# Two-layer decoder trunk on one core: norms summed block by block through PSUM banks, and attention's projection units placed in late row blocks and at head ends

## The reference, cut to what matters

```python
mod = silu(c) @ ada_w[l] + ada_b[l]          # sh1, sc1, g1, sh2, sc2, g2
h = rmsnorm(x, norm_g[l, 0]) * (1 + sc1) + sh1
y = even_mixer(h, ...) if l % 2 == 0 else odd_mixer(h, ...)
x = x + (1 + g1) * rmsnorm(y, norm_g[l, 1])
h = rmsnorm(x, norm_g[l, 2]) * (1 + sc2) + sh2
y = (silu(h @ w_gate) * (h @ w_up)) @ w_down
x = x + (1 + g2) * rmsnorm(y, norm_g[l, 3])
```

## Time and profile before

| | us |
|---|---|
| three runs | 2991.14 to 2992.17 |
| their median | 2991.62 |
| the profiled execution | 2992.33 |
| its span in the profile | 2990.6 |
| mean granted clock of PE | 0.947 of full |

### The profile page before, as it was taken

How to read it: one execution, slowest core, us unless ns; L and a number is a source line. 1 busy time by engine, 2 the same in 40 slices (tenths; PEclk the granted TensorE clock), 3 DMA queues, 4 the chain that set the end, 5 groups by cost and what they waited for, 6 DMA issues and landing times.

```text
span 2990.6 us, 35461 instructions
## 1 busy us (share of the span) xinstructions
PE 2687.0 (90%) x12576; PEld 2193.1 (73%) x12576; DVE 1261.9 (42%) x1451; ACT 1071.0 (36%) x1610; POOL 967.4 (32%) x402
## 2 busy tenths in 40 slices
PE   4999999989899999999999997666889999999995
PEld 2777778767678887788877786554667888788884
DVE  5566644333720155201567413766473005430145
ACT  2444443343433333333332223544343333322222
POOL 0111110004344444344434443211334444344442
PEclk7999999999899999999999998888999999999998
DMA  6233332043223332232346543111222333233232
GB/s 235 64 99 105 107 92 78 29 167 101 71 84 98 97 93 91 84 98 92 98 134 225 185 160 106 43 56 42 71 71 87 96 98 98 84 98 97 92 99 91
DMA packets 91097, 300.38 MB, mean 100 GB/s; under 512 B 9793, under 2 KB 10113, under 8 KB 91009
## 3 DMA queue, kind: packets, MB, share of 16 engines
q1 hardware_dynamic: 91008, 299.20, 31.4%
HBM read 275.05 MB, written 24.12 MB: 100 GB/s over the span
## 4 chain that ended last, share of the span: by engine, by line
issue 57%; PE 27%; POOL 11%; DVE 2%; DVEq 1%; ACT 1%; POOLq 1%; ACTq 0%
POOL w_lo L462 10%; PE ps L503 6%; PE ps L504 6%; PE ps L507 6%; PE ps L774 3%; PE ps L780 3%; PE ps L777 3%; POOL ybuf L473 1%; POOL arena L473 1%; DVEq L1222 0%; POOLq L476 0%; DVEq L1494 0%; DVE h_lo L1194 0%; ACT w_hi L828 0%; DVE ybuf L1186 0%
## 5 line engine op out<-in xcount | busy, mean ns | idle before, releaser
L462 POOL TENSOR_TENSOR w_lo<-w_raw,w_hi 128x1024 fp32r<-128x1024 f32 x370 | 909.4, 2461 | 1797.6 <-ACT w_hi L828 1293.5
L503 PE MATMUL ps<-h_hi,w_hi 128*128 128x512 f32 x2448 | 991.0, 405 | 85.8 <-ACT w_hi L828 54.7
L504 PE MATMUL ps<-h_lo,w_hi 128*128 128x512 f32 x2448 | 977.5, 399 | 0.0
L503 PEld LDWEIGHTS ps<-h_hi,w_hi 128*128 128x128 f32 x2448 | 474.6, 194 | 216.8 <-issue 78.3
L507 PE MATMUL ps<-h_hi,w_lo 128*128 128x512 f32 x2448 | 606.9, 390 | 0.0
L828 ACT ACTIVATE w_hi<-w_raw 128x1024 fp32r<-128x1024 f32 x346 | 363.9, 1057 | 632.0 <-PE ps L507 320.8
L504 PEld LDWEIGHTS ps<-h_lo,w_hi 128*128 128x128 f32 x2448 | 475.7, 194 | 97.0 <-issue 0.5
L507 PEld LDWEIGHTS ps<-h_hi,w_lo 128*128 128x128 f32 x2448 | 461.5, 189 | 96.4
L1598 DVE TENSOR_TENSOR arena<-arena,ps 128x512 f32 (+1 forms) x88 | 60.5, 688 | 782.6 <-PE ps L507 782.6
L1613 DVE TENSOR_TENSOR a_lo<-arena,a_hi 128x512 fp32r<-128x512 f32 x88 | 211.6, 2404 | 212.8 <-ACT a_hi L1149 212.5
L774 PE MATMUL ps<-a_hi,w_hi 128*128 128x512 f32 x704 | 174.3, 390 | 6.6 <-ACT a_hi L1149 6.6
(11 more groups left out here) (174 smaller groups left out, 2267.8 us busy)
## 6 DMA issues: line engine op xcount, KB each, us to landing
w_raw<-weights SPq DMA_DIRECT2D x370, 512.0 KB, 3.5
arena<-ada_w SPq DMA_DIRECT2D x80, 512.0 KB, 3.6
proj<-arena SPq DMA_DIRECT2D x24, 512.0 KB, 3.4
x<-xT SPq DMA_DIRECT2D x4, 2048.0 KB, 11.1
arena<-ada_w SPq DMA_DIRECT2D x4, 2048.0 KB, 20.2
arena<-proj SPq DMA_DIRECT2D x8, 1024.0 KB, 4.8
arena<-proj SPq DMA_DIRECT2D x8, 512.0 KB, 4.1
y_hi_d<-a_hi SPq DMA_DIRECT2D x7, 512.0 KB, 2.6
```

The costliest lines, as they stand in the source:

```text
L462: pool.tensor_tensor(w_lo[:, s, :], w_raw[:, s, :], w_hi[:, s, :].bitcast(f32), ALU.subtract).then_inc(lo_done, 1)
L503: pe.matmul(bank(b), w, high[:, k, :], start=k == 0, stop=False)
L504: pe.matmul(bank(b), w, low[:, k, :], start=False, stop=False)
```

## The change

- **Norms.** ACT squares each block of 512 columns into banks 6 and 7 in turn (`squares`); DVE adds each bank into acc_b (`sums`) and signals that it was read; block k waits until block k-2 was read. A square of x waits for its pair of blocks to be updated. `update` goes in four pairs: two scalar_tensor_tensor y·gain·rinv into banks 4 and 5, then one add of 1024 columns to x; `scaled` is gone. In the hosted stages the squares of the pre norm move from hook 3 to hooks 2 and 3, four blocks each; the second half of the update and sums 0 to 3 stand at DVE's hook 2, in that order.
- **Out.** ACT copies w_hi for unit m+2, squares and evicts all eight banks; POOL sums the squares (`out_norms`); DVE does reciprocal, update, sums and h. The post mean stands after unit 0 and the pre mean after unit 4 of half 1.
- **Down.** The first row begins with banks 4 to 7 and waits for free banks before bank 0; the last row goes bank by bank, three matmuls each, and signals each bank. After FFN(1,1) ACT squares banks as they finish, DVE adds, and the last update is shared by DVE and POOL.
- **Attention.** Chunks 0 to 3 stay in rows 0 to 3; chunk 4 is cut into three parts of 8 matmuls in rows 5, 6 and 7; chunk 5 stands whole after weigh(7). Scores 0 and 1 of the next block come before `turn_out`, `turn_v` after it. `ada_turn` of blocks 1 to 6 becomes a column after each matmul pair of chunk 0 of a later block. DVE's ada steps leave rows 0 and 1 and stand doubled in rows 2 and 3.

```diff
+                for half in range(2):
+                    done = 2 * layer + half
+                    for m in range(KB):
+                        use = USE_OUT[layer] + KB * half + m + 2
+                        lo(use, use % 2)
+                        if m:
+                            pool.wait_ge(ysq_done, 8 * done + m + 1)
+                            pool.tensor_tensor(acc_y[half], acc_y[half], sq_tile[m % 2], ALU.add).then_inc(ysq_read, 1)
+                            pool.drain()
+                    pool.drain().then_inc(yacc_done, 1)
...
+                    if ada is not None:
+                        ada_column(ada, k)
...
+            def chunk_part(c, part):
+
+                u, half = chunk_of(c)
+                if part == 0:
+                    chunk_bank_free(c)
+                    pe.wait_ge(hi_done, u + 1)
+                if part == 2:
+                    pe.wait_ge(lo_done, u + 3)
+                w, h = ((w_hi, hh), (w_hi, hl), (w_lo, hh))[part]
+                for k in range(KB):
+                    mm = pe.matmul(bank(7), w[:, u % 2, k * P:(k + 1) * P], h[half][:, k, :],
+                                   start=part == k == 0, stop=part == 2 and k == KB - 1)
+                if part == 2:
+                    mm.then_inc(ch_done, 1)
...
+                if m == 0:
+                    pe.wait_ge(acc_done, n + 1)
+                    pe.wait_ge(mod_done, n)
+                    pe.wait_ge(o_done, 8 * n + 1)
+                mm = pe.matmul(bank(6)[:, ADA_COL + m:ADA_COL + m + 1], acc_one[:, m * P:(m + 1) * P], ones[:, 0:1], start=True, stop=True)
+                if m == KB - 1:
+                    mm.then_inc(ada_mm, 1)
...
                                 mean(*post[0])
-                            if pre and (i, s) == (PAIRS_OUT - 1, 0):
+                            if pre and (i, s) == (2, 0):
                                 mean(*pre)
...
-                pe.wait_ge(ssum_done, n - 1)
+                if kind == 1:
+                    pe.wait_ge(yacc_done, 2 * layer + half + 1)
+                else:
+                    pe.wait_ge(bsum_done, 10 if (layer, kind, half) == (1, 3, 1) else square_site(layer, kind, half) + 1)
                 pe.wait_ge(root_done, n)
-                pe.matmul(bank(7), mean_w[:, :], rinv[:, rinv_slot(kind, half), :], start=True, stop=True)\
+                pe.matmul(bank(7), mean_w[:, :], acc_y[half] if kind == 1 else acc_b, start=True, stop=True)\
                     .then_inc(mean_done, 1)
...
+                        if n == 7 and not last:
+                            chunk_part(ahead + 4, 2)
                         if n:
...
                         turn_weights(n)
+                        if n == 7:
+                            chunk_part(ahead + 4, 2)
                         if n:
                             weigh(n - 1)
...
-                    if n < 6 and not last:
-                        chunk(6 * (b + 1) + n)
-                        if (b, n) == (6, 5):
-                            pe.drain().then_inc(unit_used, 24)
+                    if not last:
+                        if n < 4:
+                            chunk(ahead + n, b if n == 0 and 0 < b < 7 else None)
+                        elif n in (5, 6):
+                            chunk_part(ahead + 4, n - 5)
+                if not last:
+                    scores(0, b + 1, 1 - slot)
                 weigh(7)
                 if not last:
-                    turn_v(b + 1, before(LANE[kind]))
-                    scores(0, b + 1, 1 - slot)
+                    for part in range(3):
+                        chunk_part(ahead + 5, part)
+                    if b == 6:
+                        pe.drain().then_inc(unit_used, 24)
+                    scores(1, b + 1, 1 - slot)
                 turn_out()
+                if not last:
+                    turn_v(b + 1, before(LANE[kind] + 1))
...
+                def row(i, s, order=range(KB), first=False):
                     u = use + 2 * i + s
                     slot = (use + s) % 2
...
-                    for m in range(KB):
+                    for m in order:
+                        if first and m == 0:
+                            pe.wait_ge(free0, tiles + 1)
+                            pe.wait_ge(free1, tiles + 1)
                         pe.matmul(bank(m), w_hi[:, slot, cols[m]], a_hi[:, s, :], start=first, stop=False)
...
+                def last_row():
+
+                    u, slot = use + FB - 1, (use + 1) % 2
+                    pe.wait_ge(hi_done, u + 1)
+                    pe.wait_ge(ah_done, FB * (d + 1))
+                    pe.wait_ge(al_done, FB * (d + 1))
+                    pe.wait_ge(lo_done, u + 3)
+                    for j, m in enumerate(LAST_BANKS if d == 3 else range(KB)):
+                        pe.matmul(bank(m), w_hi[:, slot, cols[m]], a_hi[:, 1, :], start=False, stop=False)
+                        pe.matmul(bank(m), w_hi[:, slot, cols[m]], a_lo[:, 1, :], start=False, stop=False)
+                        pe.matmul(bank(m), w_lo[:, slot, cols[m]], a_hi[:, 1, :], start=False, stop=True)\
+                            .then_inc(dn_done if j < KB - 1 else unit_used, 1)
+
+                row(0, 0, (4, 5, 6, 7, 0, 1, 2, 3), True)
+                row(0, 1)
...
+            def squares(layer, kind, half, first=0, last=KB):
+
+                site = square_site(layer, kind, half)
+                if kind == 3:
+                    a.wait_ge(dn_ev1, 4 * (dn_idx(layer, half) + 1))
+                    a.drain()
+                for k in range(first, last):
+                    if kind != 3 and k % 2 == 0:
+                        a.wait_ge(x_part, 4 * upd(layer - (kind == 0), 3 if kind == 0 else 1, half) - 3 + k // 2)
+                    if 8 * site + k > 1:
+                        a.wait_ge(sq_read, 8 * site + k - 1)
+                    src = y3[:, k, :] if kind == 3 else x[:, k, half * HALF:(half + 1) * HALF]
+                    a.activation(bank(6 + k % 2), src, ACT.Square).then_inc(sq_done, 1)
...
-                    put(1.5 if phase == "out" else 3, square, *pre, None)
-                    put(2.5 if phase == "out" else 5, root, *pre)
+                    put(2, squares, *pre, 0, 4)
+                    put(3, squares, *pre, 4, 8)
+                    put(5, root, *pre)
...
-                        if n < 7 and not last:
+                            exps(b, n + 1)
+                        if n < 5 and not last:
...
-                        if n in (5, 7) and b < 6:
-                            hi_u(3 * b + 6 + n // 6)
-                        if n == 7 and b == 6:
-                            hi_at(USE_OUT[0], 0, 0)
-                            hi_at(USE_OUT[0], 0, 1)
+                        if n == 5 and b < 6:
+                            hi_u(3 * b + 6)
...
+                    copies(7)
                     output(6)
-                    copies(7)
+                    if not last:
+                        evict(6 * (b + 1) + 4)
                     output(7)
                     if kind == 0:
                         a.drain()
                         a.activation(ms, ms, ACT.Sqrt, bias=eps_c, scale=1.0 / P).then_inc(sub_root, 1)
                     if not last:
-                        copy_v(b + 1, before(LANE[kind]))
+                        exps(b + 1, 0)
+                        evict(6 * (b + 1) + 5)
+                    if b < 6:
+                        hi_u(3 * b + 7)
+                    elif b == 6:
+                        hi_at(USE_OUT[0], 0, 0)
+                        hi_at(USE_OUT[0], 0, 1)
                     if 0 < b < HEADS - 1:
                         a.wait_ge(y_stored, 32 * b)
                     for half in range(2):
...
                                      **({} if kind else {"scale": sub_g})).then_inc(y_hi, 1)
+                    if not last:
+                        copy_v(b + 1, before(LANE[kind] + 1))
...
+                    for m in range(KB):
+                        a.wait_ge(unit_used, base + m + 3)
+                        hi_next(base + m + 2)
+                        if 0 < m < 3:
+                            if job:
+                                a.wait_ge(ysq_read, 7 * job)
+                        elif m:
+                            a.wait_ge(ysq_read, 7 * job + m - 2)
+                        a.activation(sq_tile[m % 2] if m else acc_y[half], bank(m % 4), ACT.Square).then_inc(ysq_done, 1)
+                        a.activation((y3, y_out1)[half][:, m, :], bank(m % 4), ACT.Copy).then_inc((free0, free1)[m % 2], 1)
+                        if half and m in (0, 4):
+                            root(layer, 1 + m // 4, 0)
+                        if half and m in (2, 3):
+                            squares(layer, 2, 0, 4 * m - 8, 4 * m - 4)
+                        if half and m > 4 and layer == 0:
+                            for k in ((0,), (1, 2, 3), (4, 5, 6, 7))[m - 5]:
```

(86 more changed lines are left out.)

283 lines of the change are left out of this document (120 added, 163 removed).

## The result

| | before | after |
|---|---|---|
| median of the runs, us | 2991.89 | 3063.35 |
| lowest to highest of four | 2991.14 to 2992.84 | 3056.33 to 3072.36 |
| profiled execution / its span | 2992.33 / 2990.6 | 3072.36 / 3070.6 |

The ratio is 1.024, with a 95% interval of 1.0213 to 1.0267: slower, as forecast, but by 71 us and not by 42, and outside the range of 3000 to 3062. Medians are taken over undisturbed runs alone: one of att_only's four took 6640.79 us, and without it att_only stands at 3033.97, where the expectations written before say 3036.9.

What follows compares the result with a forecast made beforehand. PE, busy 90% of the span, was taken as the bound, so only what stops or slows it costs time. Norms 72 - down 12 - 6.6 - tail 13.5 + out 0 + attention 2 = +42, giving 3034 us; range 3000 to 3062.

Steps and rivals of the forecast that it cites:

- rival (4): Attention: late rows bring the clock down too, 4 us a block, 28 in all, giving 3060 us; chance 0.14.
- Norms in hosted stages: FFN(0,0), (0,1), (1,0) and in(1,0): new stops of PE and lost clock, +19.05 per FFN site, +15 for in, +72 us together.
- A: Hosted stages, hook 2: PE stops at unit 5's end while ACT's square waits for DVE's sum; 11.0 us, bounds 9.6 and 12.5.
- the 1.4 for a late DVE: Part of A: 1.4 us added because DVE, slowed beside POOL, reaches unit 5 only just in time.
- B: Hosted stages, hook 3: the same stop again, with only the multiply of units 6 and 7 ahead of sum 4; 4.05 us.
- Clock after A and B: Hosted stages: PE's clock falls after both stops, losing 4.3 us after A and 2.1 after B, 6.4 a site.
- The wait behind hook 1: in(1,0): PE's present wait of 4.07 us shrinks to the 1.8 that FFN has, -2.2 us.
- Down: Down stages: waits and slow clock at the ends go, -12 us (or -8); waits at the four starts go, -6.6.
- Tail: After the last matmul: 33.0 us shrink to about 19.3, -13.5 us, bounds -10 and -16.
- Out: Out stages: a pre-mean wait of 6 to 8 us replaces 6.2 removed, FFN start shortens; 0 over both, bounds -5 and +5.
- Attention: Seven attention blocks: late-row waits against filled head ends and 2 to 2.5 us of clock back a block; +2, bounds -8 and +12.
- The five waits that the prediction lists: Attention, kind 0 block: 2 us each in rows 4 and 6, 0.5 in rows 5 and 7, 1.75 before v's turn; given as 8.3.

Runs made afterwards that it cites:

- att_only: The kernel before with only the attention part of the change: 3033.97 us, ratio 1.0134.
- norms_only: The changed kernel with attention left as in the kernel before; all norm, out, down and tail edits stay: 3020.84 us, ratio 1.0084.
- att_ada: The kernel before with only the modulation edits (columns inside chunk 0, no group at the block's end, DVE's steps moved): 3033.13 us, ratio 1.0134.
- att_turn: The kernel before with the whole attention part, but the modulation columns as a group at the block's end, after the turn of v: 3007.43 us, ratio 1.0046.

## Why the prediction was right or wrong

The forecast of +42 met 71 through two errors of opposite sign: the norm, out, down and tail edits were put 12 us too high, attention 39 too low. That 3063 lies only 1 us over the range is no merit of the range: its upper edge came from rival (4), whose cause is not the one found.

**Norms in hosted stages: mechanism right, size too large.** Predicted +72 less 18.6 for down and 13.5 for the tail, 0 for out: +40. norms_only measures +28. Two terms were mis-sized, 1.4 and 2.4 us in each of four sites.
- A was put at 11.0 and is 9.55 (9.48 to 9.55 in the four sites). The failed term is the 1.4 for a late DVE. B was 4.05 and is 3.9 to 4.0.
- Clock after A and B was put at 6.4 a site. From late squares against early ones a site in FFN(0,1) is worth 17.5, 13.5 of it stops, so 4.0. The 4.3 after A was taken from the FFN start behind the wait of 7.60 us, where all 24 matmuls ran at half clock (10.57 us, some with short stops for h_lo between them). After A only the first eight did, for 3.5 us, and the window of 12.60 us loses 1.8:

```profile
1257.30:1269.90 12.60, 12.56 (x48) 10.13 (x48) 0.00 (x0) 2.45 (x4) 4.70 (x2) 0.86 0.28 83
```

- in(1,0) stopped for 9.48 and 3.86, not 12.5 and 4.05. The wait behind hook 1, forecast to shrink from 4.07 to 1.8, is 3.25.

**Down: right.** The ends cost no wait and run at full clock. FFN(1,1), which hosts nothing, shows starts and the clock after an end by themselves: 245.7 us of gate and up before, 242.4 after, 3.3 less as 1.6 + 1.7 said; the step from a down's first matmul to the next stage's first fell by 2.3.

**Tail: nearly right.** -11.4 for -13.5, within its bounds; POOL's adds (1.38) and the last steps were longer than taken.

**Out: right by cancellation.** From the first matmul of the stage to the first of the FFN, out(0) grew by 2 us and out(1) shrank by 2 (114.3 to 112.2); forecast 0 over both, bounds -5 to +5. In out(0) PE's wait for the pre mean is 8.8 us, where 6 to 8 was forecast (5.1 in out(1)), and the FFN start waits 3.7 in place of 7.60:

```profile
PE ps L639 <- DVEq L1309: 8.8, 1, 8.8
```

The collisions that the Trainium skill's rule ("SBUF — State Buffer", section "Who interferes with whom") speaks of are in the chain behind that wait: two STTs of the update, which read two operands from SBUF, take 4.55 us beside POOL's w_lo and new add (L504, which itself takes 1.75 in place of 1.30), and 1.42 in FFN(0,1) above without POOL. The add with one PSUM input keeps its 1.22 us beside POOL's w_lo at 789.30, and the sums beside it take 1.48 the two. The trace agrees with the rule:

```profile
774.64 2.39 POOL L476 TENSOR_TENSOR w_lo<-w_raw,w_hi 128x1024 fp32r<-128x1024 f32 x1 [3.95 <-ACT w_hi L973]
774.75 4.55 DVE L1346 SCALAR_TENSOR_TENSOR ps<-ybuf,gain,rinv 128x512 f32<-128x512 f32 x2 [0.17 <-issue]
...
776.99 1.75 POOL L504 TENSOR_TENSOR arena<-arena 128x512 f32<-128x512 f32 x1
...
789.19 1.22 DVE L1350 TENSOR_TENSOR x<-x,ps 128x1024 f32<-128x1024 f32 x1
789.30 2.36 POOL L476 TENSOR_TENSOR w_lo<-w_raw,w_hi 128x1024 fp32r<-128x1024 f32 x1 [5.11 <-ACT w_hi L973]
...
790.51 1.48 DVE L1305 TENSOR_TENSOR arena<-ps,arena 128x512 f32<-128x512 f32 x2
```

**Attention: wrong.** +2 with bounds -8 to +12 was forecast, +41 measured. The step that failed is a term that the sum does not have: the narrow modulation matmuls were taken from the head end, whose new chunk "removes its waits", and their new place in chunk 0 was given no price, which is to put it at nothing without a reason. It costs 41 us alone (att_ada) and 26 within the whole part. The rest, the late rows and head ends, cost 14 in all (att_turn), 2 over the upper bound. There the waits were right: 8.3 us for a block of kind 0 was forecast, and PE idles 8.34 in the one shown under att_turn. (The five waits that the prediction lists add up to 6.75, not 8.3; with its own list the sum would have been 6 us lower, further off.) What failed there is the clock, forecast to give back 2 to 2.5 us a block: it stands at 0.93 in this block, 71.94 us long, as it did in the 68.40 before, and behind row 4's wait, 3.31 us where 2 was forecast, 12 matmuls ran at half clock. PE's waits for the biased scores over all of attention were 10.8 us before; in the changed kernel and in att_ada:

```profile
PE ps L674 <- DVE small L1491: 25.9, 17, 3.3
```

```profile
PE ps L637 <- DVE small L1404: 25.1, 19, 2.5
```

Rival (4), low clock in late rows, 3060, came nearest to the time by number, but not by cause: most of the loss was in row 0 and at the head end in front of it.

## What to carry to other kernels

Before work is moved away from a place, ask what waits there: a group of small matmuls that costs 3.4 us may stand in a wait of 2.5 us and be nearly free, and where it goes to it may cost all of that and more. When a long instruction is cut into a ping-pong through two buffers, each block inherits whatever stands ahead of its partner on the other engine; put the engine that feeds the critical one last in each hand-over (here squares one hook later), so that the other one waits. Price a lost clock from a place whose work behind the wait is the same: after a wait of 9.55 us in a dense stream it was back after 3.5 us, at an FFN start with short stops it stayed low for 10.6.
